# Gate weights cut beside the up half, and a new order of units ahead of a seven-product FFN, in a two-layer decoder trunk in split fp32

## The reference

```
def layer(x, p, buf, h0):
    x = x + 0.5 * swiglu(rms_norm(x, n_ffn1), w_ffn1_gate, w_ffn1_up, w_ffn1_down)
    mix, v, new_buf, hT = hybrid_mix(rms_norm(x, n_mix), buf, h0, ...)   # ends in concat(y_a, y_b) @ w_out
    x = x + mix
    x = x + 0.5 * swiglu(rms_norm(x, n_ffn2), w_ffn2_gate, w_ffn2_up, w_ffn2_down)
    gate = sigmoid(rms_norm(x, n_ple) @ w_ple_gate)
    return x + gate * (p @ w_ple_proj)                # the "PLE" stage

def swiglu(x, wg, wu, wd):
    return (silu(x @ wg) * (x @ wu)) @ wd             # 1024 -> 2816 (22 tiles of 128) -> 1024
```

## Time and profile before

| | |
|---|---|
| median of 3 runs | 1999.06 us (1995.28 to 2002.83) |
| the profiled execution, its own time | 2009.22 us |
| its span, from first to last instruction | 2007.4 us |
| busy: PE, DVE, ACT, POOL | 95%, 66%, 45%, 10% of the span |
| TensorE's mean granted clock | 0.984 of full speed |

### The profile page before, as it was taken

How to read it: one execution, slowest core, us unless ns; L and a number is a source line. 1 busy time by engine, 2 the same in 40 slices (tenths; PEclk the granted TensorE clock), 3 DMA queues, 4 the chain that set the end, 5 groups by cost and what they waited for, 6 DMA issues and landing times.

```text
span 2007.4 us, 37482 instructions
## 1 busy us (share of the span) xinstructions
PE 1906.4 (95%) x15280; PEld 1872.2 (93%) x15280; DVE 1315.3 (66%) x1889; ACT 894.1 (45%) x1271; POOL 197.0 (10%) x247
## 2 busy tenths in 40 slices
PE   8999999999989999999889999999998999999997
PEld 7999999999989989999888989999998999999996
DVE  6444434578687577577877567577777775766775
ACT  5222312454455354354555354344544553534443
POOL 1000000130100000001200000013202000000012
PEclk9999999999989999999989999999999999999998
DMA  5232222322345354454245354462223444544431
GB/s 203 86 103 85 93 87 93 114 76 75 95 116 143 106 127 141 102 144 134 74 106 134 111 126 145 99 175 97 74 96 95 121 142 100 132 127 115 137 125 47
DMA packets 63690, 225.83 MB, mean 112 GB/s; under 512 B 7152, under 2 KB 9488, under 8 KB 63552
## 3 DMA queue, kind: packets, MB, share of 16 engines
q1 hardware_dynamic: 52576, 184.87, 27.5%
q0 software_dynamic: 10976, 38.98, 10.9%
HBM read 221.52 MB, written 2.31 MB: 111 GB/s over the span
## 4 chain that ended last, share of the span: by engine, by line
PE 65%; DVE 12%; DMA 9%; ACT 8%; issue 5%; POOL 0%; DVEq 0%; SPq 0%; ACTq 0%; POOLq 0%
PE main L596 32%; PE main L736 10%; PE main L632 9%; DMA raw<-weights_dram 8%; PE aux L632 4%; PE aux L736 4%; PE aux L888 2%; ACT w_hi L1031 2%; DVE w_lo L1370 2%; ACT w_lo L1025 2%; ACT w_hi L984 1%; ACT wx L1041 1%; DVE x L1622 1%; DVE tau L1478 1%; DVE tmp L1544 1%
## 5 line engine op out<-in xcount | busy, mean ns | idle before, releaser
L596 PE MATMUL main<-part_hi,w_hi 128*128 128x260 f32 x1888 | 382.4, 284 | 3.4 <-DVE tmp L1643 1.5
L596 PE MATMUL main<-part_hi,w_lo 128*128 128x260 f32 x1888 | 380.1, 283 | 0.0
L596 PE MATMUL main<-part_lo,w_hi 128*128 128x260 f32 x1888 | 379.3, 282 | 0.0
L1370 DVE TENSOR_TENSOR w_lo<-raw,w_hi 128x1024 fp32r<-128x1024 f32 (+1 forms) x194 | 245.8, 1269 | 86.5 <-ACT w_hi L984 82.6
L984 ACT ACTIVATE w_hi<-raw 128x1024 fp32r<-128x1024 f32 (+1 forms) x212 | 218.0, 1033 | 187.2 <-PE main L736 84.7
L632 PE MATMUL main<-part_hi,w_hi 128*128 128x260 f32 x792 | 235.9, 298 | 65.8 <-DVE tmp L1544 44.1
L596 PEld LDWEIGHTS main<-part_hi,w_hi 128*128 128x128 f32 x1888 | 291.6, 188 | 5.8 <-issue 3.4
L596 PEld LDWEIGHTS main<-part_hi,w_lo 128*128 128x128 f32 x1888 | 290.6, 188 | 0.0
L596 PEld LDWEIGHTS main<-part_lo,w_hi 128*128 128x128 f32 x1888 | 290.0, 188 | 0.0
L632 PE MATMUL main<-part_lo,w_hi 128*128 128x260 f32 x792 | 228.9, 289 | 0.0
L632 PE MATMUL main<-part_hi,w_lo 128*128 128x260 f32 x792 | 228.6, 289 | 0.0
(11 more groups left out here) (253 smaller groups left out, 3665.0 us busy)
## 6 DMA issues: line engine op xcount, KB each, us to landing
raw<-weights_dram SPq DMA_DIRECT2D x344, 512.0 KB, 3.4
w_lo<-weights_dram POOLq DMA_DIRECT2D x66, 512.0 KB, 5.4
x<-x_in_dram SPq DMA_DIRECT2D x4, 520.0 KB, 7.1
y_out<-x SPq DMA_DIRECT2D x8, 260.0 KB, 2.7
mix<-p_in_dram POOLq DMA_DIRECT2D x2, 520.0 KB, 3.8
tau<-ln_dram POOLq DMA_DIRECT2D x2, 512.0 KB, 4.0
tau<-ws_dram POOLq DMA_DIRECT2D x2, 512.0 KB, 4.7
bs<-bs_dram POOLq DMA_DIRECT2D x2, 256.0 KB, 4.1
```

The source lines that it names most:

```text
L596: last = pe.matmul(ps[:, q, 0:HALF], ww[:, s, w], xx[:, k, q * HALF:(q + 1) * HALF], start=(a == 0 and b == 0), stop=(a == kts - 1 and b = ...
L1370: dve.tensor_tensor(w_lo[:, s, 0:c], raw[:, s, 0:c], w_hi[:, s, 0:c], ALU.subtract).then_inc(wlo, 1)
```

## The change

Four things change. (1) In `gate_cut`, ACT writes the negated copy first and the high part second, with a counter of its own (`gate_hi`) that P1 and `tau4` wait for. (2) Inside a chunk, the gate cut of tile g+2 is moved on ACT from the end of turn g-1 (ahead of `copy_p5` and `hi12`) to the start of turn g, behind `hi_b`; at a chunk's end the low part of the second down unit moves on DVE behind `h_lo`. (3) The output and PLE units are ordered 0, 4, 1, 5, 2, 6, 3, 7, on the host's side too, so that sigma(k) can be done after every second unit, and the places of the sigma tiles in the shared buffer are changed to allow it; the cut of the PLE input `p` moves from o = 2 to o = 0 and 1. (4) `rstd` stands on DVE ahead of `lo_b`, `tau1` and `tau2` of the first tile. The additions of squares stay on POOL. The diff, cut to its core:

```
+ORDER = tuple(k for h in range(XT // 2) for k in (h, h + XT // 2))
...
     def P1(t):
...
+        pe.wait_ge(gate_hi, S + t + 1)
         pe.wait_ge(gate_lo[gate_slot(t)], 16 * ((S + t) // 2 + 1))
-        kw = (lambda k: pe.wait_ge(xlo, XT * stat + k + 1)) if first and t == 0 else None
+        kw = (lambda k: pe.wait_ge(xlo, XT * stat + 2 * k + 1)) if first and t == 0 else None
...
             def gate_cut(n, t, T_):
                 act.wait_ge(raw_in[n % SLOTS], 16 * (n // SLOTS + 1))
-                act.activation(w_hi[:, gate_slot(t), :], raw[:, n % SLOTS, :], ACT.Copy)
                 act.activation(w_lo[:, gate_slot(t), :], raw[:, n % SLOTS, :], ACT.Copy,
                                scale=-1.0).then_inc(gate_neg, 1)
+                act.activation(w_hi[:, gate_slot(t), :], raw[:, n % SLOTS, :], ACT.Copy).then_inc(gate_hi, 1)
...
                     copy_u2(1)
-                    gate(3)
                     copy_p5(1)
                     hi12(n + 4, S + 2)
                     for g in range(1, tiles - 1):
                         act.wait_ge(unit, n + 2 * g)
                         hi_b(n + 2 * g, S + g)
+                        gate(g + 2)
                         copy_p1(g + 1)
                         h_hi(g - 1)
                         done(g, "P4")
                         hi34(n + 2 * g + 2, S + g + 1)
                         silu(g)
                         copy_u2(g + 1)
-                        gate(g + 3)
                         copy_p5(g + 1)
                         if g + 2 < tiles:
                             hi12(n + 2 * g + 4, S + g + 2)
                     t = tiles - 1
                     hi_b(n + 2 * t, S + t)
                     h_hi(t - 1)
+                    gate(t + 2)
                     silu(t)
...
                     for o in range(XT):
                         function(G0 + G_PG + o, ACT.Sigmoid, T(0), T(1))
-                        if o > KH:
-                            sigma_hi(4 * l + 4, o - KH - 1)
+                        if o and o % 2 == 0:
+                            sigma_hi(4 * l + 4, o // 2 - 1)
                         if o == XT - 1:
                             table(ACT.Sqrt)
                         if o < XT - 3:
                             hi(N + U_PG + o + AHEAD, (o + AHEAD) % 4)
...
                     lo12(n, S)
                     if first:
                         sigma_lo(stat, KH - 1)
+                        rstd(stat)
                     lo_b(n, S)
                     tau1(n + 2, S + 1)
                     tau2(n + 2, S + 1)
                     c11(0)
-                    if first:
-                        rstd(stat)
                     c11_r(0)
...
                             down_lo(0)
-                            down_lo(1)
                     t = tiles - 1
                     c12(t - 1)
-                    lo_b(n + 2 * t, S + t, 3)
+                    lo_b(n + 2 * t, S + t, 2)
                     c22(t)
                     hidden(t - 1)
                     h_lo(t - 1)
+                    lo(d + 1, 1)
                     c21(t)
...
                 for o in range(XT):
                     dve.wait_ge(unit, N + U_OUT + o + 1)
...
-                    if o > KH:
-                        sigma_lo(4 * l + 2, o - KH - 1)
+                    if o and o % 2 == 0:
+                        sigma_lo(4 * l + 2, o // 2 - 1)
                     seven_x_lo(4 * l + 2, o)
-                    if o >= KH:
-                        sigma(4 * l + 2, o - KH)
+                    if o % 2:
+                        sigma(4 * l + 2, o // 2)
...
                     scaled(T(0), main_slot(G0 + G_PG + o), evac)
                     if o and l + 1 < DEPTH:
                         seven_x_lo(4 * l + 4, o - 1)
-                        if o > KH:
-                            sigma(4 * l + 4, o - 1 - KH)
+                        if o % 2 == 0:
+                            sigma(4 * l + 4, o // 2 - 1)
```

More of the change, by code:

```diff
@@ L246, in trunk @@
         gate_neg = sem("gate_neg")
+        gate_hi = sem("gate_hi")
         gate_lo = [sem(f"gate_lo{b}") for b in range(2)]
@@ L1315, in _ @@
                         seven_ahead(o, N + U_F2, first_tile(l, 1))
-                    if KH <= o < XT - 1:
-                        sigma_hi(4 * l + 2, o - KH)
+                    if o % 2 and o < XT - 1:
+                        sigma_hi(4 * l + 2, o // 2)
                 ffn(l, 1, U_F2, G_F2)
```

89 lines of the change are left out of this document (47 added, 42 removed).

## The result

The changed kernel takes 2006.62 us (median of 6, 2005.67 to 2010.74); the kernel before, on the same chip, 1998.65 us. The ratio is 1.0046, 95% interval 1.0031 to 1.0062: slower by 8 us, where 1950 us were forecast.

A forecast was written before the change was run, and what follows sets the result against it. PE, busy 95% of the span, was taken to bound the kernel through its own waits. Terms -47.5 - 2.2 - 3.6 + 2.8 + 0.6 = -49.9 us, from the median 1999.1, gave 1949.2, rounded up to 1950; 8-in-10 range 1940 to 1976.

The forecast's parts named there:

- The ring of before: Inside chunks: `tau4`, load, gate cut, `hi12`, `lo12`, `c22`, `lo_b`, `tau3`, `tau4` outlasts PE's work, making 38 waits, 34.9 us.
- The step that failed: Inside a chunk's turn: the moved gate cut's accumulating DMA lands at 8.1 us, 2.0 us before P1 needs it.
- the up-half ring: Inside chunks: `lo_b`, load, `tau1`, `tau2`, `hi12`, `lo12`, `c22`, `lo_b` takes 9.4 us with a 3.5 us load, under the turn.
- The term -47.5: Nine chunks: all 38 waits, their restarts and two half-clock stretches go, 47.5 us saved.
- The forecast's check by bandwidth: Each turn: three 512 KB transfers, 1.57 MB at 211 to 276 GB/s, need 5.7 to 7.5 us and barely fit in 7.
- A: Rival, inside chunks: loads and accumulation collide, P1 waits in each of 38 turns, 29 us, total 1979; chance 0.12.
- B: Rival, up-half ring: loads over 5.3 us on average make turns longer than the old 11.16 us, total 2016; chance 0.04.
- C: Rival, boundaries: the new order costs more than seen, +5.8 and +5 us, total 1961; chance 0.10.
- E: Rival, more gain: the 2.04 us waits fall too and boundaries shorten, 12 us more, total 1938; chance 0.08.
- D: Rival, inside chunks: `tau1` behind the up half's load holds `hi12`, not the gate cut; 3 us gained, 1996; chance 0.04.
- The boundaries: Starts of the FFNs and chunk ends: -2.2 us first, +2.8 second, -3.6 third, +0.6 at chunk ends.
- The base: Start of the sum: the median of before, 1999.1 us, not its profiled execution's 2009.2, which was 10.2 us above it.

The follow-up runs named there:

- e12: Changed kernel with the gate cut back at its old place, and `lo_b`, `tau3` and `tau4` earlier on DVE: 1978.25 us, 0.9899 of before.
- e3: Changed kernel with the accumulating DMA cut to 64 of 1024 columns, so another output: 1947.05 us, 0.9685 of before.
- e8: Changed kernel with the accumulating DMA in two halves, and `lo_b`, `tau3` and `tau4` earlier on DVE: 1954.11 us, 0.9729 of before.
- e11: Changed kernel with `lo_b` first in DVE's turn and `tau3`, `tau4` behind `lo12`, so only the up half's slot comes free earlier: 1955.06 us, 0.9786 of before.
- e15: e11 plus the accumulation in two halves and, in the PLE stage, the weights' high part ahead of sigma's: 1945.32 us, 0.9684 of before.
- e4: e3 plus a full accumulating DMA into the squares' buffer, which nobody waits for inside a chunk: 1959.30 us, 0.9743 of before.
- e7: Changed kernel without accumulating DMAs; GpSimd computes the gate weights' low part by subtraction: 1973.08 us, 0.9827 of before.

## Why the prediction was wrong

**The ring of before** (right). Of the 38 waits for `c22` inside chunks (34.9 us) 3 are left (1.0 us), by moving the cut; e12 shows that its old place keeps 17 of them. The turn without stalls is 10.1 us, and inside chunks e3, e8, e11 and e15 gain 586.2 - 536.5 = 49.7 us where 47.5 were forecast.

**The step that failed** is "which lands 5.4 us after the earlier trace rows: 8.1. P1 of that tile starts at 10.1, so 2.0 us are left", with its twin "with 3.5 us for the load it takes 9.4 us". Both take a landing time from rows of before, where the accumulation ran over 3 us ahead of both loads, and put it into a turn in which the change itself starts all three within 1.6 us. Measured there: 7.1 (8.4 from the start to P1 in the turn shown) and 6.5 us. With 6.5 instead of 3.5 the up-half ring is 12.4 us, over the turn; with 7.1 the accumulation has 0.3 us left at best, and it starts later than laid out since the ring delays the cut. The term -47.5 came out as +3.6.

The size of the ring is less sure than its sign. The prediction doesn't say how its 9.4 us add up; the parts named in the expectation for e4 come to 4.7 us without the load, which makes 8.2 with 3.5 and 11.4 with the up loads' mean of 6.7. The full turns behind a chunk's first two lasted 11.8 us on average. The forecast's check by bandwidth came out low too: it gave 5.7 to 7.5 us for the 1.57 MB, and in the turn shown they took 9.5 us from the first issue to the last landing, at a mean of 168 GB/s (8.2 and 8.5 us in the turns from 726.8 and 762.8):

```profile
738.34:747.82 9.48, 7.03 (x56) 6.86 (x56) 5.31 (x10) 3.70 (x7) 0.85 (x1) 0.97 0.67 168
```

**The rivals.** A named the place and the mechanism: e3 and e11 take away traffic or coincidence, and the stall goes. The Trainium skill (DMA: Bandwidth & Descriptors, "Issuing engines are not separate DMA queues") says that DMAs started by different engines run on the same 16 DMA engines and interleave; the traces agree, with up loads of 6.7 us on average beside the accumulation in after and 3.3 in e11. A's price was about half: 29 us were written, and it was 53.3 us over 48 full turns, nearly all of it in those behind a chunk's first two. 36.6 us of that are P1's waits; nearly all the rest is restarts and the half clock behind long waits, which wasn't in the price. B said "more than 5.3 us on average", and the average was 6.7 for the 30 up loads from a chunk's second turn on. I had them as two cases with 0.12 and 0.04; they are one, since a late up load delays the next accumulation, and the window of 276 GB/s at 0.99 share already spoke for it. C and E did not occur: the boundaries gained more than forecast. D was wrong about before, where `tau1` idled only 8.3 us, but what it describes, `hi12` held by `tau1` behind the up half's load, is what the changed kernel does, with a result 10 us above D's 1996.

**The boundaries** (right within 2 us; of the second FFN's two times 0.8 us were lost ahead of it, so the stage itself cost 0.8 instead of 2.8). P1(1) at 556.42 (556.0 forecast), P4(0) at 569.78 (569.2), the new wait of 3.00 us at PLE's last unit, P1(1) at 1010.07 (1011.3), P4(0) at 1023.42 (1024.6). Sum of all but the chunks: -6.6 where -2.4 was forecast; the chunk's end cost nothing, and 1.0 us went behind the last P3, which no term had.

**The base.** The difference was put on the median of before, and the traces differ by -2.9 us where the medians differ by +8.0. The cause of these 11 us is open; they don't change the verdict on the step.

## What to carry to other kernels

When a change moves the start of a transfer, its landing time is no constant any more: write down when every other transfer of the turn starts, and take the time from a stretch with the same overlap. If none exists, price the margin with the sum of the bytes at the rate of a whole turn (here 168 to 192 GB/s, not the 211 and 276 of a short window), not with the lone transfer. And when a ring is cut, compute every other ring at the longer landing time: the cure here (e11) was to put `lo_b` first in the turn, with `hi_b`, `c22`, `lo12` and `hi12` following suit. It spread the same transfers over 4.3 us and made the ring shorter.

## What the runs showed of the hardware

- Two loads and an accumulation of 512 KB each lengthen each other by how close they are issued. All within 1.8 to 1.9 us (26 turns of after, chunks' second turns on): accumulation 6.7 to 8.2 us, loads 6.2 to 7.8. Within 2.5 to 2.6 us (4 turns): 5.0 to 5.2 and 5.1 to 6.6. Over 4.3 us with the up load first (e11, 30 turns): accumulation 5.2 to 6.3, up load 3.1 to 4.4. Over 4.5 us with the accumulation first (before, 30 turns): 5.1 to 5.6, and up load 3.2 to 5.6.
- An accumulation of 32 KB took 4.6 us beside one of 512 KB (e4) and 2.3 us with none beside it (e3), both medians of the stretch 718 to 770.
- A GpSimd subtraction of 128x1024 takes 2.7 us on average (176.2 us in 66). A DVE addition of two SBUF tiles begun 0.56 us behind its start takes 2.87 to 2.90 instead of 0.69 us and ends 0.55 us behind its end, in all of 29 turns (e7).
